# The down weights of a mixture of experts: from SyncE's DMA queue to ScalarE's

## The reference, cut to what matters

```python
def expert_block(args):
    xb, e = args
    return (jax.nn.silu(xb @ we_gate[e]) * (xb @ we_up[e])) @ we_down[e]
```

## Time and profile before

| | before |
|---|---|
| median of 3 executions | 1486.5 us |
| the profiled execution, its own time | 1488.43 us |
| its span in the trace | 1486.7 us |
| TensorE busy in the span | 1351.9 us (91%) |
| VectorE busy | 1046.8 us (70%) |
| ScalarE busy | 613.1 us (41%) |
| GpSimd busy | 347.0 us (23%) |

### The profile page before, as it was taken

How to read it: one execution, slowest core, us unless ns; L and a number is a source line. 1 busy time by engine, 2 the same in 40 slices (tenths; PEclk the granted TensorE clock), 3 DMA queues, 4 the chain that set the end, 5 groups by cost and what they waited for, 6 DMA issues and landing times. The chain is left out here.

```text
span 1486.7 us, 18817 instructions
## 1 busy us (share of the span) xinstructions
PE 1351.9 (91%) x5795; PEld 926.4 (62%) x5795; DVE 1046.8 (70%) x1651; ACT 613.1 (41%) x931; POOL 347.0 (23%) x350
## 2 busy tenths in 40 slices
PE   5799999974889799996899999999999999999947
PEld 3577677632779444443676776767767677676713
DVE  4539999968753253363688888888888888888617
ACT  3322212134224211212465655656656566565502
POOL 0243424233000000001222232322323223232200
PEclk9799999887789899998899999999999999999969
DMA  8434443210000461133599999999999999998358
GB/s 303 153 135 149 177 163 114 85 71 0 2 1 1 193 240 77 64 142 152 222 342 357 344 357 353 359 344 349 376 393 358 347 344 354 355 355 293 133 221 351
DMA packets 85266, 339.26 MB, mean 228 GB/s; under 512 B 16918, under 2 KB 20176, under 8 KB 58084
## 3 DMA queue, kind: packets, MB, share of 16 engines
q1 hardware_dynamic: 65400, 304.97, 54.5%
q0 software_dynamic: 19584, 33.60, 6.2%
q10 hardware_dynamic: 236, 0.09, 0.0%
HBM read 332.31 MB, written 44.04 MB: 253 GB/s over the span
## 5 line engine op out<-in xcount | busy, mean ns | idle before, releaser
L2158 DVE TENSOR_TENSOR gate_up_low<-gate_up,gate_up_high 128x1024 fp32r<-128x1024 f32 x204 | 244.7, 1220 | 42.2 <-ACT gate_up_high L2049 42.2
L2130 PE MATMUL py<-down_ring,hT 128*128 128x512 f32 x544 | 250.0, 602 | 0.9 <-ACT hT L2068 0.9
L2091 PE MATMUL p_gate_up<-gate_up_high,x_hi 128*128 128x512 f32 x544 | 242.7, 446 | 5.3 <-DVE x_lo L2167 5.3
L2091 PE MATMUL p_gate_up<-gate_up_low,x_hi 128*128 128x512 f32 x544 | 217.1, 399 | 0.0
L2091 PE MATMUL p_gate_up<-gate_up_high,x_lo 128*128 128x512 f32 x544 | 215.9, 397 | 0.0
L2049 ACT ACTIVATE gate_up_high<-gate_up 128x1024 fp32r<-128x1024 f32 x204 | 203.7, 1051 | 0.6 <-PEq L1308 0.6
L2130 PEld LDWEIGHTS py<-down_ring,hT 128*128 128x128 f32 x544 | 98.0, 190 | 98.8 <-issue 98.7
L2020 POOL TENSOR_TENSOR carrier<-offsets 1x1 f32<-1x1 f32 x136 | 29.2, 215 | 522.1 <-DVE tokens L2176 475.2
L269 POOL TENSOR_TENSOR ring_lo<-ring,w_hi 128x2048 fp32r<-128x2048 f32 x19 | 91.5, 4814 | 179.3 <-ACT w_hi L310 179.3
L2091 PEld LDWEIGHTS p_gate_up<-gate_up_high,x_hi 128*128 128x128 f32 x544 | 104.1, 191 | 45.1 <-issue 21.4
L429 PE MATMUL pz<-h_hi,w_hi 128*128 128x512 f32 x304 | 123.4, 406 | 7.7 <-DVE h_lo L497 7.7
(11 more groups left out here) (359 smaller groups left out, 2038.2 us busy)
## 6 DMA issues: line engine op xcount, KB each, us to landing
down_ring<-in_we_down SPq DMA_DIRECT2D x68, 1024.0 KB, 9.6
gate_up<-in_we_gate SPq DMA_DIRECT2D x51, 1024.0 KB, 7.0
gate_up<-in_we_up SPq DMA_DIRECT2D x51, 1024.0 KB, 9.8
ring<-in_w_ada SPq DMA_DIRECT2D x12, 2048.0 KB, 7.9
ring<-in_w_in SPq DMA_DIRECT2D x9, 2048.0 KB, 10.1
x_again<-in_we_gate SPq DMA_DIRECT2D x17, 1024.0 KB, 7.0
x_again<-in_we_up SPq DMA_DIRECT2D x17, 1024.0 KB, 9.8
rows<-expert_rows SPq DMA_DIRECT2D x6, 2048.0 KB, 18.3
```

The source lines that it names most:

```text
L2091: mm = pe.matmul(pgu[u % 2][:, :], x[:, u % 2, k, :], weights, start=(k == 0 and n == 0), stop=(k == KD - 1 and n == 2))
L2130: mm = pe.matmul(py[half][:, :], hT[:, u % 2, k, :], weights[:, k, half * N:half * N + N], start=(k == 0), stop=(k == 1))
L2158: V.tensor_tensor(moe.low[u % RING][:, :, piece(i), :], moe.gate_up[u % RING][:, :, piece(i), :], exact(w_hi[:, u % 2, :, piece(i), :]), A ...
```

## The change

SP no longer loads the down weights, apart from those of block 3, which now go out first, ahead of the wait for the first free gate and up buffer. ScalarE issues the others, on a queue of its own: at the end of y_half of block b it issues the down weights of block b+4, into the buffer that block b has left. In the tail ScalarE first reads `n_blocks` and compares, and where block b+4 exists reads its expert from `blocks`.

```diff
@@ block.sync
             def weights(b, u):
                 sp.wait_ge(s_gu, b + (1 - RING))
                 moe.load_gate_up(sp, b, u)
-                if not (isinstance(b, int) and b == RING):
-                    sp.wait_ge(s_y, b - RING)
-                moe.load_down(sp, b - 1, (u - 1) % RING)
-
+
+            moe.load_down(sp, RING - 1, RING - 1)
             for u in range(RING):
                 weights(RING + u, u)
...
-            sp.wait_ge(s_y, NE - RING)
-            moe.load_down(sp, NE - 1, (NE - 1) % RING)
...
                             sp.wait_ge(s_gu, RING * turn + (u - RING + 1))
                             moe.load_gate_up(sp, expert, u)
-                            sp.wait_ge(s_y, RING * turn + (u - RING + 1))
-                            moe.load_down(sp, expert, u)
@@ block.scalar, y_half
                 act.activation(y[:, u % 2, 0:N], py[0][:, :], ACT.Copy).then_inc(s_yA, 1)
+                if first:
+                    moe.load_down(act, b + RING, u % RING)
+                else:
+                    with act.If(b + RING < act.value_load(moe.n_blocks[0:1, 0:1], min_val=NE, max_val=MAXB)):
+                        expert = act.value_load(moe.blocks[0:1, 0, bass.ds(b + RING, 1)], min_val=0, max_val=NE - 1)
+                        moe.load_down(act, expert, u % RING)
```

## The result

The changed kernel takes 1494.11 us (median of 8 executions, 1491.99 to 1494.65), the kernel before in executions beside it 1490.05 (8 executions, 1485.4 to 1492.65). The three executions behind the 1486.5 us above are among these eight. The ratio of the two kernels is 1.0034, with a 95% interval of 1.0019 to 1.0048. Taken by the ratio that is 5.1 us more, between 2.8 and 7.1; the two medians differ by 4.1. The profiled execution took 1492.41 us with a span of 1490.6.

What follows compares the result with a forecast made beforehand. TensorE's work was taken to bound the steady step. Steady steps 0, tail 3.7 and start 1.5 sum to 5.2 us, so the median 1486.5 becomes 1491.7 us, 0.35% slower; range 1485.5 to 1498.

Steps and rivals of the forecast that it cites:

- What bounds: Steady steps: TensorE busy all 590 us, step 10.31 us; no engine waits for weights, so earlier landing is worth nothing.
- Two loads at once: Rival: two queues drawing weights slow the transfers; 10% longer would make 57 steps 27 us longer, 1519 us; chance 0.04.
- ScalarE in the steady steps: Steps 0 to 59: one DMA issue and register instruction a step, mostly hidden behind the copy of y; 0 us.
- D: ScalarE's added delay between y and the first high part; taken as 0.15 us in steady steps, bounds 0 to 0.8.
- the cover: Slack on the path ScalarE, VectorE, TensorE before TensorE loses time: 0.37 us before the silu and little more.
- The rival of an unhidden issue: Steady steps: ScalarE's issue isn't hidden behind the copy; at D = 0.8 up to 12 us, 1497 to 1504; chance 0.13.
- The one test in the prediction: Entering the tail in the kernel before: the rule gave 1.07 us lost, the trace showed 1.13 more than 10.31.
- ScalarE in the tail: After y of blocks 60 to 63, two register reads and the issue, D = 1.7; tail 3.7 us, bounds 2 to 6.
- VectorE's own register reads for these blocks cost it 0.50 and 0.68 us: Tail: VectorE's added time, taken as 0.68 us after block 61 and 0.5 elsewhere.
- the rule: TensorE loses D plus VectorE's added time minus 0.37 us, less the loss of the step before; never below zero.
- The start: First gather beside the fourth down load lands after 8.8 us instead of 7.1; + 1.5 us, bounds 0 to 2.5.
- The rule on register reads: ScalarE's tail reads: a floor of about 600 ns each would add some 1 us; measured 482 and 274 ns were used.

Runs made afterwards that it cites:

- one read a step: Changed kernel plus one unused read of `n_blocks` on ScalarE behind each DMA issue of steps 0 to 59; ratio to the kernel before 1.0079.
- the tail by SP: Changed kernel, but SP again issues the down weights of blocks 64 to 67; ratio to the kernel before 1.0007.
- The run with the old order: Changed kernel, but SP issues block 3's down weights behind block 4's gate and up loads, as before; ratio to the kernel before 1.0034.
- the load ahead of y: Changed kernel, but ScalarE issues the down load of block b+3, reads included, before waiting for py of block b; ratio to the kernel before 1.0000.
- held loads: First down loads wait for TensorE's first turn of gathered rows: on the kernel before, 0.9974; on the load ahead of y, 0.9977 (ratios to the kernel before).
- one read fewer: Changed kernel, but ScalarE's tail compares with the block count read on entering instead of rereading `n_blocks`; ratio to the kernel before 1.0024.

## Why the prediction was right, and where it was off

The forecast was 0.35% slower, within what can be told from no change; measured is 0.34% (0.19 to 0.48).

*What bounds.* Right: TensorE's work sets the steady step (in the tail it doesn't, see below), nothing waits for weights, and an earlier landing of the down weights (9.0 instead of 9.7 us) is worth nothing. The step from y of 0 to y of 59 is the same to 0.03 us in 609. Two loads at once cost the transfers nothing, so that rival falls.

*ScalarE in the steady steps.* Right: D was taken as 0.15 and is 0.18, the issue hides behind the copy, and the wait before the silu shrank as forecast. Not foreseen was the turn of the loop with D = 0.45, which is above 0.37 and still inside the cover. The rival of an unhidden issue at D = 0.8 was priced at 12 us; one read a step, with D = 0.73 and 1.00 at the turn, costs 4.1. The cover was mis-sized: it is 0.7 us, not "0.37 us before the silu and little more". The one test in the prediction didn't show this. It set 1.07 against 1.13 us between two first weight loads, but from y to y the step behind that delay took 11.11 us, 0.8 too long, and a cover of 0.7 gives 0.94 + 0.50 - 0.7 = 0.74.

*ScalarE in the tail.* Right in kind, its size off: 3.7 us forecast, 5.7 measured, within the bounds of 2 to 6. ScalarE's delays were right: 1.92 us from y to high on entering, where D = 1.4 meant 1.9, and then 2.37, 2.07, 2.07 and 2.55 us from y to high where about 2.2 was forecast (with the read of `n_blocks` shorter and the gaps longer), and hiddenT of the last block came 1.30 us after y instead of 0.54, 0.76 us later where 0.6 was forecast. Two steps failed. The first is "VectorE's own register reads for these blocks cost it 0.50 and 0.68 us": after blocks 59 to 62 it idled 0.41, 0.99, 1.49 and 1.12 us (before: 0.50, 0.30, 0.68 and 0.30). Its second read of `blocks` grew, in these two rows of before and of after:

```profile
L2187 DVEq TENSOR_LOAD <-blocks x4: 300/305/322, 1346.7 to 1377.5; - x4
```

```profile
L2187 DVEq TENSOR_LOAD <-blocks x4: 314/886/1131, 1345.2 to 1380.0; - x4
```

With that, VectorE's one-hot table is late as well, and TensorE waits at a second place in each of these steps, ahead of down, which the rule doesn't know:

```profile
PEld pid L2119 <- DVE hot L2191: 1.9, 4, 0.7
```

No such wait stands in the tail of the kernel before. Where it stands, the step is no longer as long as TensorE's work: it is a closed chain through three engines. From y of block 60 (1351.06, with high at 1353.43 and the column copy at 1357.88, shown above) to y of block 61:

```profile
1354.53 2.36 DVE L2158 TENSOR_TENSOR gate_up_low<-gate_up,gate_up_high 128x1024 fp32r<-128x1024 f32 x2 [2.17 <-ACT gate_up_high L2043]
...
1358.76 0.17 PEld L2119 LDWEIGHTS pid<-column,hot 128*128 128x128 bf16 x4 [0.53 <-DVE hot L2191]
...
1362.92 0.60 ACT L2067 ACTIVATE y<-py 128x512 f32<-128x512 f32 x1 [3.38 <-PE py L2130]
```

That is 2.37 us from y to high, 1.10 to VectorE's low parts, 2.36 for two of these, 0.99 of VectorE's reads, and 5.04 from the column copy through the table and down to the next y: 11.86. Without the first term and the reads it is 8.50 us, and it is 8.48 to 8.52 in all 19 steps of the tail, in six kernels, in which TensorE waits for the table. So once y to high and the reads together pass 1.8 us (10.31 - 8.50), a step loses all that is above. This is the second step that failed, the rule's "less what it lost in the step before": a loss ahead of down puts y itself off, and nothing is taken off. The rule gave 1.5, 0.3, 1.7, 0 and, after block 63, 1.7 us, times 0.8; between first weight loads the steps lost 1.50, 1.55, 1.75, 1.37 and, after block 63, nothing (10.21 us). The 1.7 us that didn't come after block 63 paid for a part of what was forecast too low, so the tail as a whole was off by only 2 us.

ScalarE's delay is enough to bring this wait on: in the run with the tail by SP, VectorE's reads on entering are short (0.47) and ScalarE is late (1.93), TensorE waits 0.34 us ahead of down, and the step is 1.93 + 0.47 + 8.51 = 10.91 us. Of the tail's 5.7 us, VectorE's longer reads then make up about 2.2 (4.01 us in four steps instead of 1.78), an estimate from these rows; no run keeps them short in all four steps.

*The start.* Right: 1.5 us forecast from the steady landing of 8.8; the gather landed after 8.6 instead of 7.1. That y of block 0 came 1.3 us later behind the first high part agrees, but that stretch varies by up to 2.3 us between kernels that start alike. The run with the old order brought the gather back to 7.28, and holding the down loads to 4.5 to 4.7.

*The sum.* The stretches give 7.0 us, the times 5.1 (2.8 to 7.1), the forecast 5.2. So the closeness of forecast and time is in part luck: the tail was 2 us dearer than reckoned, and the measured time cannot tell 5.2 from 7.0.

*The rule on register reads.* The Trainium skill (DMA: Bandwidth & Descriptors, Latency and other measured facts) gives about 600 ns as the floor of such a read. On ScalarE they took 0.28 us, the first one 0.48 (one more of 0.55 and one of 0.72 stand in two of the runs), so the measured values decide: the rule would have overpriced ScalarE's side. On VectorE single reads did reach 0.9 and 1.1 us.

*Queues.* The same page (Issuing engines are not separate DMA queues) says that issuing on several engines saves only the time of issuing. The runs agree: with the load ahead of y the ratio is 1.0000, and held loads gain as much with SP alone (0.9974) as with both (0.9977).

## What to carry to other kernels

A DMA issue on a computing engine is nearly free where it stands behind a dispatched instruction, or where the engine waits anyway, and costs its full length elsewhere: with the same queue, moving the issue and its reads ahead of a wait of 2.6 us took away all of the tail's 5.7 us. How much a wait covers is measured by lengthening the delay until steps lose time, and by reading the steps one by one: the mean over all steps hides that only one in four lost. And a rule found on one step holds only as long as the engines meet in the same place; here a second wait, ahead of down, took over. Before a load is moved to another queue, ask whether the queue that had it is short of time; SP waited 497 of 590 us. The gain was elsewhere: three loads, the first of which was needed 25 us after the first turn (704.30 to 729.35), stood beside the one gather that TensorE was waiting for, and holding them back gave 0.26% for two moved lines and a wait.

## What the runs showed of the hardware

The queue of ScalarE goes on with a DMA issue while a copy that it has dispatched still runs: in the first steps the issue starts in the same 0.01 us as the copy, at 731.23, and high still follows by 0.49 us.

A read of the one-element `n_blocks` takes 0.47 to 0.57 us the first time on each engine and 0.28 on ScalarE afterwards; most reads of `blocks` take 0.26 to 0.41. Only with ScalarE late in the tail do VectorE's reads of `blocks` grow, up to 1.36 us. This stands in the changed kernel and in the runs with one read fewer, with the start as before and with reads in each step; it is absent in the kernel before and in the five runs with high 0.5 us behind y in the tail. Single long reads do occur there on other engines: 0.55 and 0.72 us on ScalarE, 0.68 on SP. What holds these reads up stays open.

The clock after the first gather adds chance, and it is why the stretch up to y of block 0 differs between kernels that start alike. In the 28 us after the first turn the granted clock was 0.74 in the kernel before and 0.87 in the run with one read fewer, that is between the levels of 1.2 and 2.4 GHz, with a larger share at the upper one; and y of block 0 came 25.9 us after the first turn there instead of 28.8. Such 2.9 us are more than most terms of this study.
